# Gated linear attention moved in among the units of the input projection of a hybrid decoder layer

## What is computed

```python
h = rmsnorm(x, norm_g)
proj = h @ w_in                      # 1024 x 3218 columns
(g_q, g_k, g_v, g_lr, g_gate, f_q, f_k, f_v, f_fg, f_gate, m_q, m_gate) = split(proj)
log_a = log_sigmoid(g_lr @ w_alpha_up + b_alpha) / 16
# linear attention, 4 heads, 48 key and 96 value channels, chunks of 64 tokens
b = cumsum(log_a, within a chunk)
q_dec, k_dec, k_to_end = q*48**-.5*exp(b), k*exp(-b), k*exp(b_last - b)
o = (tril(q_dec @ k_dec.T)) @ v + q_dec @ S ;  S = exp(b_last)*S + k_to_end.T @ v
o_gla = rmsnorm(o, gla_norm_g) * silu(g_gate)
o_mem = softmax(m_q @ mk.T / 8) @ mv * silu(m_gate)          # 4 heads, 256 memory tokens
o_fox = softmax(f_q @ f_k.T / 8 + c_t - c_s, causal) @ f_v * silu(f_gate)   # 6 heads
out = rmsnorm(x + concat(o_gla, o_fox, o_mem) @ w_out, final_norm_g)
```

## Time and profile before

| | us |
|---|---|
| three runs: median (lowest to highest) | 1478.14 (1477.81 to 1480.31) |
| span of the profiled execution, the time that the rows below add up to (no time of its own beyond the span is given) | 1480.9 |
| TensorE busy in it | 1312.8 (89%) |
| VectorE, ScalarE, POOL busy | 665.6, 576.9, 411.6 |

### The profile page before, as it was taken

One profiled execution on the slowest core, in us unless ns is written; L12 is line 12 of the kernel. 1 busy time (PEld: TensorE's weight loads), 2 busy tenths in 40 slices (PEclk: granted clock), 3 DMA queues, 4 the chain that ended last, 5 costly groups with the idle time before them and its releaser, 6 DMA issues. The chain is left out here.

```text
span 1480.9 us, 20787 instructions
## 1 busy us (share of the span) xinstructions
PE 1312.8 (89%) x6576; PEld 1053.3 (71%) x6576; DVE 665.6 (45%) x1606; ACT 576.9 (39%) x1154; POOL 411.6 (28%) x408
## 2 busy tenths in 40 slices
PE   5898989999999999938785985999899999599997
PEld 4887878888888888814453663777678687478886
DVE  4563311110000011178874763888788798432222
ACT  3563201111111000047652874777677777421010
POOL 5223420111111011044553577222322422300000
PEclk9999999999999999959876987999999999799999
DMA  5453333331222121165321543422623520355553
GB/s 201 144 164 118 111 111 113 127 120 64 70 78 78 64 78 58 49 177 166 109 85 60 165 113 84 115 93 61 156 63 94 122 59 12 98 207 198 199 174 137
DMA packets 98908, 166.45 MB, mean 112 GB/s; under 512 B 10740, under 2 KB 51444, under 8 KB 96996
## 3 DMA queue, kind: packets, MB, share of 16 engines
q1 hardware_dynamic: 96088, 156.97, 34.7%
q10 hardware_dynamic: 2560, 8.39, 1.4%
q0 software_dynamic: 192, 0.33, 0.1%
HBM read 101.36 MB, written 64.29 MB: 112 GB/s over the span
## 5 line engine op out<-in xcount | busy, mean ns | idle before, releaser
L644 PE MATMUL col_cps<-h_T,tok_slot 128*128 128x512 f32 x2112 | 481.6, 390 | 4.0 <-POOL tok_slot L600 3.9
L644 PEld LDWEIGHTS col_cps<-h_T,tok_slot 128*128 128x128 f32 x2112 | 397.9, 188 | 87.8 <-issue 4.9
L1736 PE MATMUL out_yps<-out_w,out_mix 128*128 128x512 f32 x768 | 177.7, 394 | 19.3 <-DMA out_mix<-scr_mix 16.8
L1736 PEld LDWEIGHTS out_yps<-out_w,out_mix 128*128 128x128 f32 x768 | 145.7, 190 | 51.1 <-DMA out_mix<-scr_mix 17.1
L1540 ACT ACTIVATE fox_pT<-fox_tps 128x512 fp32r<-128x512 f32 x240 | 124.8, 531 | 88.2 <-PE fox_tps L1473 85.5
L1578 DVE TENSOR_SCALAR_CACHE_REDUCE fox_prob<-fox_sps 128x512 f32<-128x512 f32 (+2 forms) x240 | 142.0, 606 | 36.6 <-PE fox_sps L1463 33.7
L1589 DVE TENSOR_TENSOR fox_pT<-fox_tps,fox_pT 128x512 fp32r<-128x512 f32 x240 | 141.6, 604 | 21.7 <-ACT fox_pT L1540 20.9
L1473 PE MATMUL fox_tps<-all_ident,fox_prob 128*128 128x128 f32 x816 | 134.6, 278 | 15.1 <-ACT fox_prob L1532 8.2
L707 DVE COPY tok_xn<-col_cps 128x512 f32<-128x512 f32 x24 | 16.6, 692 | 287.4 <-PE col_cps L644 287.4
L1486 PE MATMUL fox_ops<-fox_pT,fox_v 128*128 128x512 f32 x480 | 137.2, 376 | 0.0
L1473 PEld LDWEIGHTS fox_tps<-all_ident,fox_prob 128*128 128x128 f32 x816 | 99.9, 141 | 45.1 <-ACT fox_prob L1532 11.6
(11 more groups left out here) (189 smaller groups left out, 1760.3 us busy)
## 6 DMA issues: line engine op xcount, KB each, us to landing
scr_split<-tok_w SPq DMA_DIRECT2D x64, 256.0 KB, 2.7
out_mix<-scr_mix SPq DMA_DIRECT2D x32, 512.0 KB, 4.2
tok_xin<-in_w_cols SPq DMA_DIRECT2D x22, 512.0 KB, 3.8
tok_xin<-in_x SPq DMA_DIRECT2D x16, 512.0 KB, 3.7
scr_gates<-tok_xn SPq DMA_DIRECT2D x32, 256.0 KB, 2.3
out_x<-in_x SPq DMA_DIRECT2D x16, 512.0 KB, 6.2
out<-out_o ACTq DMA_DIRECT2D x16, 512.0 KB, 4.9
scr_fox_v<-tok_vst SPq DMA_DIRECT2D x16, 384.0 KB, 2.9
```

The lines of the kernel that those rows point to most:

```text
L644: mm = nc.tensor.matmul(cps[c][:, :], w[s][a_][:, kk, :], hT[b_][:, kk, c * CH:(c + 1) * CH], start=(kk == 0 and n == 0), stop=(kk == KT - ...
L1736: mm = nc.tensor.matmul(yps[s][:, c, :], mix[s][a][:, kk, :], w[b][:, kk, c * CH:(c + 1) * CH], start=(kk == 0 and n == 0), stop=(kk == MI ...
```

## The change

The stage of the linear attention is gone as a stage. `columns_and_linear_attention` replaces it and `project_columns`. A class `ColumnUnits` says what stands beside each of the 88 units; the loops over units are written out.

- The order of the columns is new: value (3), raw q and k (3), the gates of the linear attention (3), then the 8 split ones, then 5 gates.
- The units of the value columns (12) are made with tokens in rows: 128 tokens of `hT` are stationary and 128 columns of weights move, so a unit is 96 matmuls of 128 moving columns. The step then reads v as it needs it (`scr_gla_v`), and the transposes of v (L920) and the zero-padded copy `vz` go.
- The decays (`g_lr`, `w_alpha_up`, the running sum) are made for 512 tokens at units 6, 8, 10 and 12 and stored to `scr_gla_b`; the step reads them back, with q and k, for 128 tokens at a time.
- A step is spread over three units: at the first its scores and the last step's outputs, at the second the state and the last step's transposed outputs, at the third nothing. Steps lie at units 36 to 85.
- The projection has two PSUM banks in place of four. A state product is four matmuls of 64 rows and 192 columns, where it was two of 128 rows and 384 columns.
- The first loads of both softmax heads are issued at the start of the first softmax stage, ahead of its gate tiles, and VectorE fills their constant rows there.
- `TokenStage` places its tiles on the other side of SBUF.

```diff
+class ColumnUnits:
+    KINDS = ["value"] * 3 + ["raw"] * 3 + ["gate"] * 3 + ["split"] * NSPLIT + ["gate"] * (NGATE - 3)
+    UNITS = NCOL * NCH
+    G0 = 36
...
+    def step_at(cls, u):
+
+        n, half = divmod(u - cls.G0, 3)
+        return (n, half) if half < 2 and -2 <= n <= cls.STEPS else (None, half)
...
+    Z_UNITS = {6 + 2 * g: g for g in range(NCH)}
...
+        cps = [k.ps(f"cps{s}", [P, CH]) for s in range(2)]
...
+                for u in range(CU.UNITS):
+                    j, c = divmod(u, NCH)
+                    if c == 0 and j + 2 < NCOL:
+                        sp.wait_ge(w_lo, j + 1)
+                        sp.dma_start(w_raw[j % 2][:, :, :], w_cols[j + 2]).then_inc(cols_loaded[j % 2], 16)
+                    if u in Z_UNITS:
+                        g = Z_UNITS[u]
...
+                        sp.dma_start(lr[g % 2][:, :], scr.lr[:, g * CH:(g + 1) * CH]).then_inc(lr_loaded[g % 2], 16)
...
+                    store_unit(u)
...
+                def decay_logits(g):
+                    pe.wait_ge(lr_loaded[g % 2], 16 * (g // 2 + 1))
...
+                    if u in Z_UNITS:
+                        decay_logits(Z_UNITS[u])
+                    n, half_step = CU.step_at(u)
+                    if n is not None:
+                        if half_step == 0:
+                            if n >= 1:
+                                outputs(n - 1)
+                            if 0 <= n < NS:
+                                key_side(n)
+                        else:
+                            if 0 <= n < NS:
+                                chunk_states(n)
+                            if n >= 1:
+                                transposed_outputs(n - 1)
+                    if c == 0:
+                        pe.wait_ge(w_lo, j + 1)
+                    if u >= 2:
+                        pe.wait_ge(evacuated, u - 1)
+                    if CU.KINDS[j] == "value":
+                        for i in range(CH // P):
+                            tokens = slice((4 * c + i) * P, (4 * c + i + 1) * P)
+                            for kk in range(KT):
+                                for r, (a_, b_) in enumerate(PASSES):
+                                    mm = nc.tensor.matmul(cps[u % 2][:, i * P:(i + 1) * P], hT[a_][:, kk, tokens],
+                                                          w[j % 2][b_][:, kk, :],
+                                                          start=(kk == 0 and r == 0), stop=(kk == KT - 1 and r == 2))
...
+                for head in opening:
+                    head.first_loads(sp)
                 load_gate(0, 0)
                 load_gate(0, 1)
                 second.first_loads(sp)
...
+                for head in opening:
+                    head.first_fill(nc.vector)
```

More of the change, by code:

```diff
@@ L743, in gated_linear_attention @@
         gn = k.sb("gn", [P, 3])
+        bf = k.sb("bf", [FOX_H, 1])
+        dec = [k.sb(f"dec{s}", [KR, PAIRS, P // GLA_C]) for s in range(2)]
+        ss, ms, rstd, half = (k.sb(n, [P, GLA_H]) for n in ("ss", "ms", "rstd", "half"))
+        cps = [k.ps(f"cps{s}", [P, CH]) for s in range(2)]
+        rows_ctx = ExitStack()
+        with rows_ctx:
+            kr = Pools(nc, rows_ctx, "rows")
+            rT, a_full = kr.sb("rT", [FGLR, T]), kr.sb("a", [FOX_H, T])
+            parts = [kr.sb(f"part{i}", [FOX_H, T], F32R) for i in (HI, LO)]
+            rps = kr.ps("rps", [P, T])
@@ new lines, in columns_and_linear_attention @@
+        f, a = rT[0:FOX_H, :], a_full[:, :]
+        decay_ctx = ExitStack()
+        with decay_ctx:
+            kz = Pools(nc, decay_ctx, "decay")
+            lr = [kz.sb(f"lr{s}", [GLA_R, CH]) for s in range(2)]
+            keep, zabs, la, bz = (kz.sb(n, [KR, PAIRS, CH]) for n in ("keep", "zabs", "la", "b"))
+        q, kk_, b = ([k.sb(f"{n}{s}", [KR, PAIRS, P]) for s in range(2)] for n in ("q", "k", "b"))
+        tail, ep, em, ee, kd, kte = (k.sb(n, [KR, PAIRS, P]) for n in "tail ep em ee kd kte".split())
@@ new lines, in _ @@
+                for u in range(CU.UNITS):
+                    if u in Z_UNITS:
+                        softplus(Z_UNITS[u])
+                    n, half_step = CU.step_at(u)
+                    if n is not None:
+                        if half_step == 0:
+                            if 0 <= n < NS:
+                                copy_keys(n)
+                            if n >= 1:
+                                squares(n - 1)
+                        elif 0 <= n + 1 < NS:
+                            exponentials(n + 1)
+                    evacuate(u)
@@ L1205, in _ @@
-                split(NS - 1)
+                pool.memset(half[:, :], -0.5)
+                forget_rows()
+                reset_marks()
+                for u in range(CU.UNITS):
+                    j, c = divmod(u, NCH)
+                    if c == 0 and j >= 1 and j + 1 < NCOL:
+                        split(j + 1)
+                    if u == CLEAR_UNIT:
+                        clear_tiles()
+                    n, half_step = CU.step_at(u)
+                    if n is not None:
+                        if half_step == 0:
+                            if n >= 1:
+                                rstds(n - 1)
+                            if 0 <= n < NS:
+                                gates(n)
+                        else:
+                            if n >= 1:
+                                split_mix(n - 1)
+                            if 0 <= n + 1 < NS:
+                                decayed_keys(n + 1)
```

1048 lines of the change are left out of this document (459 added, 589 removed).

## The result

Four runs of the changed kernel took 1548.74, 1548.94, 1605.88 and 1611.14 us (median 1577.41), four of the kernel before beside them 1475.74 to 1480.31 (median 1477.97). The forecast was 1482, its range 1458 to 1508, and the kernel is slower by more than the range reaches. The profiled execution took 1548.74, its span is 1547.0 where that of before was 1480.9.

What follows compares the result with a forecast made beforehand. TensorE bounds the projection, while no engine bounds the linear attention, where four wait in turn. Terms -179.6-5.6+67.2+76.8+7.0+13.2+3.2+4+18 = +4.2 us against the 1480.9 span; carried to the runs' median, 1482 us, range 1458 to 1508.

Steps and rivals of the forecast that it cites:

- The clock falls in the value units: Rival: TensorE drops to 1.2 GHz in the twelve value units, adding 109 us, for 1590 us; chance 0.05.
- The clock after them: +3.2: Term: TensorE's clock lost after the four waits for decay products, half of 1.7 us each, +3.2 us.
- value units at full clock: Term: 12 value units of 96 matmuls at 0.115 us cost 132.5 where 65.3 stood, +67.2 us.
- decay products: Term: eight float32 matmuls of 512 columns on TensorE, 0.87 us each, +7.0 us.
- waits for `lr`: Term: TensorE waits 3.0 to 3.5 us ahead of units 6, 8, 10 and 12, +13.2 us.
- half-steps' waits: Term: 0.12 us at each of 34 half-steps among the units, +4 us, called a guess.
- steps: Term: 16 linear-attention steps on TensorE at 4.8 us, +76.8 us, from 72 to 85.
- The opening: Term: first loads ahead of gate tiles delay POOL's first gating in the memory heads to about 32 us, +18 us.
- The opening is hidden: Rival: POOL catches up in the memory heads, so the opening's 18 us vanish, for 1464 us; chance 0.15.
- The value units' price: Term at 0.115 us a matmul; rival by columns about 68 ns, or the skill's 81, for 1428 to 1445; chance 0.10.
- Half-steps wait: Rival: TensorE waits 0.7 us for a late partner at each of 34 half-steps, adding 24 us, for 1505; chance 0.17.
- from the first unit to the last 644 us, so that the memory heads begin near 791: Sign that the forecast is right: length of the columns on TensorE and start of the memory heads.

Runs made afterwards that it cites:

- the kernel with bursts: Changed kernel with `lr` loads one unit earlier and sixteen overwritten 512-column matmuls ahead of units 0, 6, 8, 10 and 12; median 1487.44 us.
- burst once: Changed kernel with `lr` loads one unit earlier and sixteen overwritten 512-column matmuls ahead of unit 0 only; median 1533.14 us.
- late products: Changed kernel with decay products at units 12 to 18 and clearing at unit 22, waits kept; 1495.64 to 1499.88 us, or 1612.4 to 1613.29.
- early loads: Changed kernel with the loads of `lr` one unit earlier; 1527.83 and 1526.6 us, or 1588.62 and 1589.04.
- the pieces: Changed kernel with early `lr` loads, each decay product cut into sixteen 64-column matmuls, and sixteen overwritten 512-column matmuls ahead of unit 0; median 1570.16 us.
- the pause: Changed kernel with early `lr`, products at units 12 to 18, overwritten wide matmuls before unit 0, TensorE waiting at unit 6 for unit 5's bank; median 1535.88 us.

## Why the prediction was wrong

**The step that failed** is the one on the rival *The clock falls in the value units*, which got 0.05, and its twin, *The clock after them: +3.2*. Against the rival the forecast held a stream of 256 columns and short runs of transposes that showed no such stretch; neither is a long stream of 128-column matmuls, and the trace of before has none. The price of the clock behind a wait was taken from a unit of 512 columns, where it is won back within a few us, and carried to units of 128, where it isn't: 3.2 us stood in the sum for what cost 59.2 in value units. The order of the instructions had the two ingredients next to each other: products with waits at units 6, 8, 10 and 12, and value units to both sides.

The rival's size, 109 us for all twelve units, was too large for the lower level, where six units made 59 (its 0.095 a matmul has no source, for doubling 0.115 would add 0.115; measured is 0.103); the runs at the upper level, with all twelve, came to 1606 and 1611 where it had 1590.

**The other terms of the columns**, against their measure:

| term | forecast | measured | from |
|---|---|---|---|
| value units at full clock | 0.115 each | 0.112, so -3.5 | 43.09/384 |
| half clock in units 6 to 11 | none | +59.2 | 576 x (0.2147 - 0.112) |
| decay products | 7.0 | 15.0 | 4 x 3.75 |
| waits for `lr` | 13.2 | 17.4 | 3.50, 5.36, 3.13, 5.42 |
| clock behind them in wide units | 3.2 | 2.4 | 133.03 less 576 x 0.2268 |
| half-steps' waits | 4 | 0 | no row |
| steps | 76.8 | 74.1 | 16 x 4.63 |

The differences sum to +60.4, and the columns came out 59.6 above the forecast (45.8 for -13.8). The two long waits are those at which the load of a column's weights stands ahead of that of `lr` in SP's list. I had allowed 0.4 to 0.6 us for issuing it, and that is what it took (0.54); but `lr`, issued behind it, landed some 1.3 us later as well (3.7 us from issue to product at 259.64, 2.3 at 209.37). The products doubled because they ran at half clock, and the trace of before had that price: the product in the earlier trace rows, also behind a wait, takes 2.01 us, and the granted clock from 636.45 to 638.40 is 0.50. The forecast took its 0.87 from records at full clock instead.

**The opening** was right in its mechanism and its first number (32 us); its size was 23.9 for 18, since the second head's loads made turn three wait too. *The opening is hidden* is refuted by its undoing, which gave 16 to 18 us.

**The value units' price**: of the rules weighed, the 81 ns that the Trainium skill (TensorE: Matmul & The Clock Gate, § Back-to-back issue gap) gives for a pair of load and matmul is not what this stream costs (112); the trace's own pair was the better guide. *Half-steps wait* is refuted: 34 half-steps, no wait.

Without the clock and the products' doubling (59.2 + 4 x 1.8) the span would have been 1480.6 by this estimate, inside the range and near the 1485.1 of the sum; the kernel with bursts, 1487 with 19 us added and the waits' 17 gone, agrees within 4 us.

**Slips in the working.** The sign "from the first unit to the last 644 us, so that the memory heads begin near 791" doesn't follow from the terms, which give 650 and 798; they began at 855.14. Waiting half-steps at 1505 count the 4 us of their term twice. Most terms came out near their measure; one missing mechanism was worth more than all their errors together.

## What to carry to other kernels

A term for the clock belongs to the form of the matmuls that follow the disturbance, not to the disturbance: before a stream of narrow matmuls, each with its own weights, is put where anything pauses or interrupts it, ask what would lift the clock again. If such a stream can't be avoided, enter it from wide matmuls and put a few (here sixteen of 512 columns) behind every break; better, keep the wide form and turn the result with a few transposes where it is used. And a kernel whose runs end at two levels has a state that something sets by chance: a burst ahead of the suspected place tells at once whether it is this one.

## What the runs showed of the hardware

- A gapless stream of 128-column fp32r matmuls, each with new weights, held either clock: 246 us at 0.50 with TensorE busy for all of it, and 64 us at 1.00. The only rises seen in it came within its first 0.6 us, behind the sixteen transposes (141.0 in the changed kernel). Each run of 512-column matmuls read here that began at 0.50 had the clock back within 6 us: 2.1 us in (burst once), 4.6 (changed kernel, at 361.68), 5.9 (late products, at 396.61). The Trainium skill (TensorE: Matmul & The Clock Gate, § What's actually happening) has it that "the default state is throttled, and activity releases the throttle"; for those 246 us the trace does not agree.
- That stream lost its clock at a pause of 0.78 us and not at one of 0.33, at an uninterrupted product of 2 us with 16 rows, and at pieces of 0.40 us, one ahead of every third matmul. Each fall stands close behind the start of the break: 3.4 us in the changed kernel, 3.7 with the early loads, 3.8 with the pieces, 1.2 with one burst, 1.0 at the pause. With sixteen 512-column matmuls right behind a product there was none.
- At half clock a value matmul takes 0.2134 us (122.94/576), which is 2 x 128 columns at 1.2 GHz, as if load and matmul added up there. At full clock it is 0.112, a little over the half.
- Ahead of the columns TensorE idles for 5.3 us and makes sixteen short transposes, at 0.50 in every profile of a kernel with such value units. Whether the clock then rises at the head of the value stream differs between executions of one program. What decides it was not tried.
- From the start of the state product to the next record it is 0.83 us for eight records of 192 columns on half of the rows (521.81 to 522.64), where it was 1.30 for four of 384 columns on all rows. So some of two row groups' work seems to run side by side, as the Trainium skill has it (TensorE: Matmul & The Clock Gate, § Part 3: Packing small matmuls). The pieces of a step add up to 5.1 us in the earlier trace rows, and these 0.47 are the greatest single part of the way from there to 4.63.
